# The row pitch of the pairs' split inputs and gated products: 448 columns or 416

## The chip, the cores and the metric

One core of one Trainium2 chip. The metric is the device time of the whole program in microseconds (us), the median of three runs. A profile is one execution, taken by the hardware profiler.

## What is computed

One layer of an encoder, in float32, applied with the same weights to 512 prompt tokens and 2048 sample tokens, each of 1024 features:

```python
h = rms(x, norm1_g)
q, k, v, c = split(h @ w_in)
attn = window_attention(rms(q), rms(k), v, sink)        # +-128 keys, ALiBi
u = silu(layernorm(dwconv31(a * sigmoid(gate))))        # a, gate = split(c)
x = x + concat(attn, u) @ w_out
h2 = rms(x, norm2_g)
g = silu(dwconv3(h2 @ ffn_w_gate) + ffn_dw_b)
x = x + (g * (h2 @ ffn_w_up)) @ ffn_w_down              # D_FF = 2816
```

What matters here is the last two lines, the feed-forward part.

## The kernel before, in words

**Splitting.** Every float32 matmul is done as three faster ones: an operand is split into a high part (a copy rounded by ScalarE, ACT) and a low part (input minus high part, by VectorE, DVE), and high x high, high x low and low x high are added up in PSUM. A matmul has a stationary operand of 128 x 128 and a moving one of 128 rows by up to 512 columns. Columns are tokens, so a tile is [128 partitions, rows of tokens], and TensorE (PE) reads one row of it per matmul.

**Stages.** The program is one list of slots of TensorE's work: projections and output products of five chunks of 512 tokens, with attention and convolution beside them, then the feed-forward part of two plain windows of 462 and 444 tokens (L2224, L2240), and from about 1483 us to the end two *pairs* of windows of TP = 414 tokens each. A window is loaded with one token more at each side, TQ = TP + 2 = 416, for the convolution over three tokens.

**The pairs.** For a pair the gate and up products of two windows, two halves of the features and two rows of weight tiles are made in Winograd's form of Strassen's scheme: seven products in place of eight. Its inputs are seven window parts, the loaded B11, B12, B21, B22 and the differences T1 to T4 (`pair_window_sum`, L1942; B12 and T3 share a buffer). Each is [128, KH = 4, TQ], split by ACT (`pair_window_high`, L1490) into `b_hi` and by DVE (`pair_window_low`, L1947) into `b_lo`. `pair_product` (L2370) makes one of the seven products: for each of four rows three matmuls, over columns 0 to 415 for the gate and 1 to 414 for up. ACT copies a product out of PSUM into `e_buf` (L1500), DVE adds others to it (L1954), then come the convolution's taps (L1963 and L1966, which read from one and two columns further on), the activation, the product of gate and up (L1978), and the split of the result into `mid2`: high part by ACT (`pair_mid_high`, L1530), low part by DVE (`pair_mid_low`, L1986). `mid2` is [128, 4 tiles, 2 parts, 2 windows, TP]. `pair_down` (L2384) multiplies it by the down weights, four or two tiles deep, and DVE adds the result to `pair_y` (L2000). Weight tiles of 512 columns are split at L1477 and L1930.

A pair is 22 groups (11 pairs of hidden tiles, gate and up) in six *passes*. A full pass is 336 product matmuls (four groups of seven products of twelve) and then 192 down matmuls.

**Order.** All four queues follow lists written by the planner for each product: `SP_AT`, `ACT_AT`, `DVE_AT` and the list of products `PROD`. They hold no address, and no size of a buffer enters them. Loads of window parts (`load_pair_window`, L942) for the second pair wait until the last group of the first pair has used the buffer; they read rows of 416 tokens from a scratch tensor in HBM where rows lie PAD_COLS apart. They share the queue of SyncE (SP) with the loads of weights (L957, L966).

**Places.** Tiles are put at offsets worked out from a base, which here is byte 7168 of the partition, a multiple of 256. The places before and after the pairs' stage overlap in time with other tiles, and two of them are maxima, in which the sizes of the pairs' buffers appear (L600 to L603):

```python
R_SM = max(R_Y + up256(4 * KT * TC), R_D + 4 * B_BYTES + 3 * E_BYTES + M_BYTES + 2 * Y_BYTES + V_BYTES)
R_HW = R_SM + up256(2 * up(4 * TH) + 2 * up(4 * TC))
R_SIDE = max(R_HW + 2 * up(4 * KT * H_PITCH), R_SM + (HI_RING + 5) * W_BYTES + 2 * V_BYTES + H)
```

With the kernel's numbers the first is max(125440, 123904) and the second max(165632, 163840). `pitch(cols)` rounds up to a multiple of 64 columns, 256 bytes. B_BYTES is the size of one window part (seven `b_lo`, which share their places with `b_raw`, and seven `b_hi`), M_BYTES that of `mid2`.

Of the kernel before, what the change touches and what calls it, by code (L numbers as in the profile page):

```python
# [45 lines left out]
TP = 414  # L46
# [6 lines left out]
TQ = TP + 2  # L53


def pitch(cols):
    return -(-cols // 64) * 64
# [473 lines left out]
def encoder_layer(nc, x, x_tok, w_in, w_out, w_ffn, w_down, w_pass, params, consts, y):  # L531
    with ExitStack() as ctx:
# [60 lines left out]
        def up256(n):  # L593
            return -(-n // 256) * 256

        B_PITCH, P_PITCH = pitch(TQ), pitch(TP)
        B_BYTES, E_BYTES, V_BYTES, W_BYTES, Y_BYTES = 4 * KH * B_PITCH, up256(4 * TQ), up256(4 * TP), 4 * KH * P, up256(4 * KT * TP)
        M_BYTES = 4 * 4 * 2 * 2 * P_PITCH
        M_PITCH, H_PITCH = pitch(TC), pitch(TH)
# [1935 lines left out]
```

## Time and profile before

| | |
|---|---|
| median of 3 runs | 2582.4 us (2579.91, 2582.4, 2582.7) |
| span of the profiled execution, first to last instruction | 2578.6 us |
| that execution's own time | not listed; its span is 3.8 us below the median |
| instructions | 35519 |
| TensorE, VectorE, ScalarE, GpSimd busy | 99%, 72%, 48%, 7% of the span |
| granted TensorE clock | 1.000 |

In a profile, PE is TensorE's matmuls, PEld its weight loads, DVE VectorE, ACT ScalarE, POOL GpSimd, SP SyncE; a q behind a name is that engine's queue. Line numbers are those of the kernel. Matmuls overlap: one of them lasts about twice the distance between two starts, so the pace is read from starts or from the chain, not from the mean of one. Tile names are given without their numbers, so `part_hi`, `T_hi` and `B_hi` each stand for several buffers.

### The profile page before, as it was taken

The page shows a single profiled execution, that of the slowest core. Times are in us where ns is not written, and L with a number is a line of the kernel's source. Part 1 is how long each engine was busy: PE and PEld are TensorE (multiplying, and loading weights), DVE is VectorE, ACT ScalarE, POOL GpSimd, SP SyncE. Part 2 cuts the span into 40 slices and gives each one's busy share as a digit, 9 for nine tenths or more (in the row PEclk, how much of TensorE's full clock was granted, in tenths as well). Part 3 has the DMA queues.
Part 4 walks back from the last instruction along what each step waited for, and adds up shares of the span by engine and source line. Part 5 has one row for each costly group of instructions (what it writes and reads, how often), then busy time and mean ns, then how long its engine had stood idle before and what let it go on. Part 6 is the DMA issues. An engine that isn't in the chain of part 4 may idle for free. (4 is left out here: it accounts for less than half of the span.)

```text
span 2578.6 us, 35519 instructions
## 1 busy us (share of the span) xinstructions
PE 2556.6 (99%) x12927; PEld 2287.9 (89%) x12927; DVE 1861.8 (72%) x3100; ACT 1250.3 (48%) x2166; POOL 184.7 (7%) x316
## 2 busy tenths in 40 slices
PE   8999999999999999999999999999999999999999
PEld 6877777788878887888888899999999999999999
DVE  4776658887888697968884687657667875765765
ACT  6345544468337844683563444335335443533532
POOL 0110021101011111110101100000000100000000
PEclk9999999999999999999999999999999999999999
DMA  9967789734554465447439542222223522221212
GB/s 350 348 229 237 261 290 345 276 112 164 205 206 137 146 246 212 162 159 263 155 122 357 178 148 68 66 60 68 66 61 116 171 66 62 66 66 61 67 58 70
DMA packets 139757, 419.11 MB, mean 163 GB/s; under 512 B 24160, under 2 KB 38880, under 8 KB 122944
## 3 DMA queue, kind: packets, MB, share of 16 engines
q1 hardware_dynamic: 113632, 317.93, 36.5%
q0 software_dynamic: 25952, 98.92, 10.0%
q8 instruction: 104, 1.70, 0.3%
q14 instruction: 69, 0.57, 0.1%
HBM read 328.01 MB, written 88.77 MB: 162 GB/s over the span
## 5 line engine op out<-in xcount | busy, mean ns | idle before, releaser
L1477 ACT ACTIVATE part_hi<-part_raw 128x512 fp32r<-128x512 f32 x396 | 247.6, 627 | 387.7 <-DMA part_raw<-w_pass_t 158.4
L2224 PE MATMUL bank<-hw_hi,weights 128*128 128x462 f32 (+3 forms) x1408 | 420.8, 373 | 0.0
L1751 DVE SCALAR_TENSOR_TENSOR cc<-win,par,cc 128x512 f32<-128x512 f32 x600 | 408.4, 745 | 0.0
L2384 PE MATMUL bank<-mid,part_hi 128*128 128x414 f32 x1408 | 376.9, 348 | 2.5 <-DVE mid L1986 2.0
L1930 DVE TENSOR_TENSOR part_lo<-part_raw,part_hi 128x512 fp32r<-128x512 f32 x396 | 271.0, 689 | 136.1 <-ACT part_hi L1477 130.6
L2175 PE MATMUL bank<-h_hi,weights 128*128 128x512 f32 x1104 | 354.6, 394 | 0.0
L2224 PEld LDWEIGHTS bank<-hw_hi,weights 128*128 128x128 f32 x1408 | 264.9, 188 | 37.0 <-issue 12.2
L2384 PEld LDWEIGHTS bank<-mid,part_hi 128*128 128x128 f32 x1408 | 263.3, 188 | 4.3 <-DVE mid L1986 3.4
L2224 PE MATMUL bank<-hw_lo,weights 128*128 128x464 f32 (+3 forms) x704 | 259.3, 368 | 0.0
L2175 PEld LDWEIGHTS bank<-h_hi,weights 128*128 128x128 f32 x1104 | 207.3, 188 | 51.2 <-issue 5.9
L2370 PE MATMUL bank<-T_hi,part_hi 128*128 128x414 f32 (+1 forms) x704 | 246.2, 350 | 0.5 <-DVE e L1954 0.5
L2370 PE MATMUL bank<-T_lo,part_hi 128*128 128x414 f32 (+1 forms) x704 | 246.0, 349 | 0.0
L2370 PE MATMUL bank<-T_hi,part_lo 128*128 128x414 f32 (+1 forms) x704 | 245.8, 349 | 0.0
L2000 DVE TENSOR_TENSOR pair_y<-bank,pair_y 128x414 f32<-128x414 f32 x192 | 111.9, 588 | 185.1 <-PE bank L2384 185.0
L2384 PE MATMUL bank<-mid,part_lo 128*128 128x414 f32 x704 | 245.0, 348 | 0.0
L1644 DVE TENSOR_TENSOR weights<-wraw,weights 128x1024 fp32r<-128x1024 f32 x154 | 187.9, 1221 | 55.6 <-ACT weights L1213 55.4
L2240 PE MATMUL bank<-mid,weights 128*128 128x462 f32 (+1 forms) x1056 | 223.9, 370 | 0.0
L2240 PEld LDWEIGHTS bank<-mid,weights 128*128 128x128 f32 x1056 | 197.1, 188 | 22.7 <-issue 5.0
L2175 PE MATMUL bank<-h_lo,weights 128*128 128x512 f32 x552 | 215.4, 390 | 0.0
L1213 ACT ACTIVATE weights<-wraw 128x1024 fp32r<-128x1024 f32 x154 | 162.9, 1058 | 93.6 <-DMA wraw<-w_down_t 67.4
L2209 PE MATMUL bank<-cat_hi,weights 128*128 128x512 f32 x640 | 204.1, 394 | 2.4 <-DMA cat_lo<-cat_scratch 2.4
L2370 PE MATMUL bank<-B_hi,part_hi 128*128 128x416 f32 (+1 forms) x528 | 184.4, 349 | 1.4 <-DVE yb L1905 1.4
(221 smaller groups left out, 4283.0 us busy)
## 6 DMA issues: line engine op xcount, KB each, us to landing
weights<-weight_scratch SPq DMA_DIRECT2D x88, 1024.0 KB, 6.0
wraw<-w_ffn_t SPq DMA_DIRECT2D x88, 512.0 KB, 3.5
part_raw<-w_ffn_t SPq DMA_DIRECT2D x176, 256.0 KB, 2.7
weight_scratch<-weights POOLq DMA_DIRECT2D x22, 1024.0 KB, 7.7
wraw<-w_down_t SPq DMA_DIRECT2D x44, 512.0 KB, 3.5
part_raw<-w_pass_t SPq DMA_DIRECT2D x88, 256.0 KB, 2.6
cat_hi<-cat_scratch SPq DMA_DIRECT2D x10, 1024.0 KB, 6.8
cat_lo<-cat_scratch SPq DMA_DIRECT2D x10, 1024.0 KB, 8.9
```

Of the source, the lines that this page charges most:

```text
L1213: nc.scalar.activation(whi[n % RING], wraw[n % RING][:], ACT.Copy).then_inc(s_whi, 1)
L1477: nc.scalar.activation(p_hi[k % HI_RING][:], p_raw[part_of(k)][:], ACT.Copy).then_inc(s_whi, 1)
L1644: nc.vector.tensor_tensor(wlo[n % RING], wraw[n % RING][:], whi[n % RING].bitcast(F32), ALU.subtract) \
L1751: nc.vector.scalar_tensor_tensor(acc, win[i][:, tap:tap + TB], w_tap, acc, ALU.mult, ALU.add).then_inc(s_cv, 1)
L1930: nc.vector.tensor_tensor(p_lo[part_of(k)][:], p_raw[part_of(k)][:], p_hi[k % HI_RING][:].bitcast(F32), ALU.subtract).then_inc(s_wlo, 1)
L2000: nc.vector.tensor_tensor(yb2[i][:, o, :], bank[BANK_Y[n % 4]][:, 0:TP], yb2[i][:, o, :], ALU.add) \
L2175: mm = nc.tensor.matmul(out[:], l[:, k, :], r[:, k, :], start=(k == 0 and i == 0), stop=(k == KT - 1 and i == 2))
L2209: mm = nc.tensor.matmul(out[:], l[:, k, :], r[:, k, :], start=(k == 0 and i == 0), stop=(k == KT - 1 and i == 2))
L2224: mm = nc.tensor.matmul(out, l[:, k, :], r[:, k, cols], start=(k == 0 and j == 0), stop=(k == KT - 1 and j == 2))
L2240: mm = nc.tensor.matmul(out, l[:, q, :], mid[:, k, part, 0:WIDTH[w]], start=(k == 0 and j == 0), stop=(k == FH - 1 and j == 2))
L2370: mm = nc.tensor.matmul(out, l[:, t, :], r[:, t, cols], start=(p in (1, 2, 5) and t == 0 and j == 0), stop=(t == KH - 1 and j == 2), skip_ ...
L2384: mm = nc.tensor.matmul(bank[BANK_Y[n % 4]][:, 0:TP], l[:, (deep * o + t) % KH, :], mid2[:, t, part, i, :], start=(t == 0 and z == 0), sto ...
```

## The change

The distance between two rows of a window part, and between two rows of `mid2`, is rounded up to 16 columns (64 bytes) in place of 64 columns (256 bytes). TQ = 416 and TP = 414 columns both had a pitch of 448 and have 416 now. The plain windows' M_PITCH and H_PITCH stay as they are.

```diff
-        B_PITCH, P_PITCH = pitch(TQ), pitch(TP)
+        B_PITCH, P_PITCH = -(-TQ // 16) * 16, -(-TP // 16) * 16
         B_BYTES, E_BYTES, V_BYTES, W_BYTES, Y_BYTES = 4 * KH * B_PITCH, up256(4 * TQ), up256(4 * TP), 4 * KH * P, up256(4 * KT * TP)
         M_BYTES = 4 * 4 * 2 * 2 * P_PITCH
```

## Rows read from the trace of the kernel before

**Rows 1.** The page: engine busy us (share) xinstructions; the granted clock in 40 slices.

```profile
PE 2556.6 (99%) x12927; PEld 2287.9 (89%) x12927; DVE 1861.8 (72%) x3100; ACT 1250.3 (48%) x2166; POOL 184.7 (7%) x316
...
PEclk9999999999999999999999999999999999999999
```

**Rows 2.** The page: the chain that ended last, share of the span by line.

```profile
PE bank L2370 24%; PE bank L2384 15%; DVE v L1978 0%; DVE part_lo L1930 0%; ACT part_hi L1477 0%; DVE mid L1986 0%; DMA part_raw<-w_ffn_t 0%; ACT mid L1530 0%; DVE e L1954 0%; DVE v L1963 0%; DVE part_raw L1921 0%; ACT v L1519 0%; DVE pair_y L2000 0%; ACT e L1500 0%; DVEq L1953 0%
```

**Rows 3.** The chain in order of time: start us, us, what, matmuls.

```profile
1639.82 63.04 PE bank L2370 x336
1702.86 35.84 PE bank L2384 x192
...
1997.65 32.99 PE bank L2384 x174
2030.64 42.70 PE bank L2370 x228
```

**Rows 4.** TensorE's waits, 1400 us to the end: us in total, times, longest.

```profile
PE bank L2384 <- DVE mid L1986: 2.0, 4, 1.0
...
PE bank L2384 <- DVE pair_y L2000: 0.5, 1, 0.5
```

**Rows 5.** Groups by shape, TensorE: count, busy us, mean ns of one.

```profile
L2384 PE MATMUL bank<-mid,part_hi 128*128 128x414 f32 x1408 | 376.9, 348 | 2.5 <-DVE mid L1986 2.0 <-DVE pair_y L2000 0.5
...
L2370 PE MATMUL bank<-T_lo,part_hi 128*128 128x416 f32 x352 | 123.5, 351 | 0.0
...
L2370 PE MATMUL bank<-T_lo,part_hi 128*128 128x414 f32 x352 | 122.5, 348 | 0.0
```

**Rows 6.** Timeline of TensorE: start us, us; firsts and lasts of stretches without a break.

```profile
1343.38 0.36 PE L2224 MATMUL bank<-hw_lo,weights 128*128 128x446 f32 x1
...
1346.98 0.36 PE L2224 MATMUL bank<-hw_lo,weights 128*128 128x446 f32 x1
...
1686.95 0.35 PE L2370 MATMUL bank<-B_hi,part_hi 128*128 128x414 f32 x1
...
1689.19 0.35 PE L2370 MATMUL bank<-B_hi,part_hi 128*128 128x414 f32 x1
...
1693.67 0.35 PE L2370 MATMUL bank<-B_hi,part_hi 128*128 128x416 f32 x1
...
1695.93 0.35 PE L2370 MATMUL bank<-T_hi,part_hi 128*128 128x416 f32 x1
```

**Rows 7.** Window parts, tile B_raw: duration ns min/median/max, first and last start.

```profile
L1490 ACT ACTIVATE B_hi<-B_raw x6: 1577/1578/1592, 1443.0 to 2011.9; 128x1664 fp32r<-128x1664 f32 x6
L1947 DVE TENSOR_TENSOR B_lo<-B_raw,B_hi x6: 1880/1885/1891, 1448.2 to 2024.6; 128x1664 fp32r<-128x1664 f32 x6
...
DMA to landing us min/median/max: 4.8/6.4/11.2
```

**Rows 8.** Lines L1477 and L1930, the same columns.

```profile
L1477 ACT ACTIVATE part_hi<-part_raw x396: 612/631/640, 1468.4 to 2560.7; 128x512 fp32r<-128x512 f32 x198
...
L1930 DVE TENSOR_TENSOR part_lo<-part_raw,part_hi x396: 679/691/695, 1482.1 to 2567.2; 128x512 fp32r<-128x512 f32 x198
```

**Rows 9.** Lines L1986, L1963 and L1966, the same columns.

```profile
L1986 DVE TENSOR_TENSOR mid<-v,mid x88: 581/583/591, 1516.2 to 2542.2; 128x414 fp32r<-128x414 f32 x88
...
L1963 DVE SCALAR_TENSOR_TENSOR v<-e,par,v x66: 643/646/650, 1498.2 to 2524.5; 128x414 f32<-128x414 f32 x66
...
L1966 DVE SCALAR_TENSOR_TENSOR v<-e,par,v x66: 650/651/653, 1498.8 to 2525.2; 128x414 f32<-128x414 f32 x66
```

**Rows 10.** Timelines of SP, ACT and DVE at the change of pairs.

```profile
1988.69 0.38 SPq L942 DMA_DIRECT2D T_raw<-h_scratch  x1
...
1997.40 1.58 ACT L1490 ACTIVATE B_hi<-B_raw 128x1664 fp32r<-128x1664 f32 x1
...
1999.59 1.88 DVE L1942 TENSOR_TENSOR T_raw<-T_raw,B_raw 128x1664 f32<-128x1664 f32 x1
...
2003.60 0.59 DVE L2000 TENSOR_TENSOR pair_y<-bank,pair_y 128x414 f32<-128x414 f32 x1 [1.63 <-PE bank L2384]
```

## The prediction

> **What bounds the kernel now.** I read the page first. TensorE is busy for 2556.6 of the 2578.6 us of the span, and its clock is at the top digit in all 40 slices [rows 1]; nothing else comes near. The chain that ended last, followed back as far as the view goes, is 24% of the span products of the pairs (L2370) and 15% down products of the pairs (L2384); no other line has as much as 1% [rows 2]. These two lines are also the only matmuls that read what the change moves. The chain in order of time says the same more sharply: a pass is 336 product matmuls in 63.04 us and then 192 down matmuls in 35.84 us, one behind the other with no other piece between them [rows 3]. TensorE's list of waits from 1400 us to the end has four entries, from 2.0 down to 0.5 us [rows 4]. So in the last 1100 us the time is the number of matmuls times the pace at which they start. There are 3696 products (six groups of 352 and six of 264) and 2112 down matmuls (1408 and 704), of which [rows 5] show three groups, 5808 together; 5808 x 187.3 ns = 1088 us.
>
> The pace: 63.04 / 336 = 187.6 ns and 35.84 / 192 = 186.7 ns [rows 3]. It follows the columns: 18 matmuls of 446 columns take 3.60 us from start to start, 200.0 each [rows 6]. Against 186.7 at 414 columns that is 0.42 ns for each column more (13.3 / 32), one period of the 2.4 GHz that the full granted clock means, and some 14 ns that do not depend on them. So reading the moving operand is on the path, and anything that slows it shows in full; there is no slack to hide it.
>
> **The change, part by part.** Only the distance between rows changes: 448 columns (1792 bytes) become 416 (1664 bytes). B_BYTES goes from 7168 to 6656, M_BYTES from 28672 to 26624. No instruction, wait, shape, buffer or queue entry is added or removed. 14 x 512 + 2048 = 9216 bytes come free, and nothing takes them. The two places where the pairs' layout could push other things, R_SM and R_SIDE, are maxima whose other term was already the larger (125440 against 123904; 165632 against 163840), so every buffer outside the pairs' stage stays where it was. Each buffer of the pairs still begins at a multiple of 256 bytes, since 6656, 26624 and the other sizes are such multiples. What is new is inside: 1664 is 6.5 x 256, so every second row begins 128 bytes past a multiple of 256.
>
> *Moving reads.* In a window part, rows 1 and 3 of four are such rows: half of the 3696 products. In mid2 the row number is (tile, part, window), so these are all rows of the second window: half of the 2112. Together 1848 + 1056 = 2904 matmuls. No row of the trace has this start, so I bound it. The nearest rows are the up products: they read columns 1 to 414, so they start 4 bytes past the multiple. 12 of them take 2.24 us, 186.7 each [rows 6], just what a down matmul with 414 columns from an aligned start takes; both forms have a mean of 348 ns [rows 5]. An odd start as such costs 0. The other end is one step of the pace seen between widths: from 414 to 446 columns, 13.3 ns, as if half a block of 256 bytes more were read; 2904 x 13.3 = 38.6 us. Even if the memory were read in whole blocks of 256 bytes, a row at offset 128 with 416 columns reaches byte 1792 and touches 7 blocks, and an aligned one touches 7 too; with 64- or 128-byte blocks the counts are 26 and 13 in both layouts. I take 0, the up products' value. Below 0: the gate products (416 columns) run at 2.26 us for 12, 188.3 ns [rows 6], where 2 columns more than 414 would explain 187.5; if the new layout brought all products to 186.7, the gain would be 3696 x 0.9 = 3.3 us. For small losses, the slowest stretch of down matmuls is 174 in 32.99 us, 189.6 ns [rows 3]; all 2112 at that pace would add 6.1 us. Both ends stay for the range.
>
> *Splitting and differences of windows.* L1490, L1942 and L1947 now see four rows that touch each other: one run of 1664 elements. If ending a row cost something, this would save it. L1947 takes 1885 ns for four rows of 416 [rows 7], L1930 takes 691 for 512 elements [rows 8]: (1885 - 691) / 1152 = 1.036 ns per element, which leaves 161 ns fixed, for one row as for four. ACT: 1578 against 631 [rows 7, 8], 0.822 per element, 210 fixed. Nothing is there to save; at most 28 splits and 8 differences in the whole kernel are touched, and the pair of windows that is split in mid-run (1997 to 2032 us) is ready without a wait of TensorE at 2030.64 [rows 3]. Term 0, cover: down matmuls of the last pass.
>
> *Writes to mid2.* L1986 takes 583 ns, 88 times, and ACT's L1530 writes the same rows just before it [rows 9]. Half will write at offset 128. For a start off the multiple the trace has VectorE's reads at 4 and 8 bytes, 646 and 651 ns, so some 5 ns [rows 9]. TensorE waited for L1986 four times, 2.0 us in all [rows 4]; 4 x 5 ns is nothing. Term 0, for the rest the cover is the products of the next group.
>
> *Window loads.* Eight transfers of 832 KB, the B ones 4.8 / 6.4 / 11.2 us from issue to landing [rows 7], now write their odd rows from offset 128. Packets stay one row, since the source rows are apart in HBM. Those of the second pair are issued before 1991 us. The tightest is B12 (loaded into T_raw, issued at 1988.69), which VectorE reads at 1999.59, 10.9 us later, without having idled [rows 10]; the first split, at 1997.40, is of B11, loaded earlier still [rows 10]. Were it 1 us late, VectorE would stand for 1 us, but 1.63 us of idle time follow before 2003.60 [rows 10]. Term 0, from 0 to 1 us. The Trainium skill speaks against the change here (DMA: Bandwidth & Descriptors, How a descriptor splits into AXI transactions): a descriptor that does not start at 256 bytes starts its first transaction at the boundary below. An estimate from its table: 56 beats for such a row in place of 52. No row here shows it for a write into SBUF; by it these loads would be some 4% longer on average, and the sum still 0.
>
> *Sum:* 0. The profiled execution has a span of 2578.6 us; its own time is not listed, and the median of the three runs, 2582.4, lies 3.8 us above that span. So 2582.4.
>
> **Rivals.** 0.2%, 5.2 us, is about what a measurement of this kernel can tell from no change.
>
> *Slower: TensorE reads a row slower when it starts 128 bytes past a multiple of 256.* Place: every second row in L2370, every second-window matmul in L2384. Price 13.3 ns on 2904, 38.6 us: 2621. It decides from 5.2 us / 2904 = 1.8 ns per such matmul. For it: reading is on the path, and no row excludes this one offset. Against it: the up products at 4 bytes pay nothing, and the block counts are equal. 0.11.
>
> *Faster: the pace of the products falls to that of the down matmuls,* 3.3 us: 2579. That alone is within 0.2%; it needs another 1.9 us, as from TensorE's idle pieces between 1981 and 1998 us. For it: gate products are 0.8 ns above what their columns explain. Against it: nothing in the change touches a column count. Over the line 0.04.
>
> *The change does not do what it says:* TQ = 416 divides by 16, TP = 414 rounds up to 416, so the pitch does fall; but had the freed bytes moved other buffers, the plain stage would shift too. The maxima above exclude it. The time would be the same, and it is in the forecast's chance.
>
> **Numbers.** Same 0.84, slower 0.12 (the rival, and 0.01 for the 6.1 us of slow down matmuls), faster 0.04. The range takes the bounds of the small unknowns around 2582.4: down by 3.3 us and the 2.5 us by which the lowest of the three runs lies below the median, 2576.6; up by 6.1 and the 1 us of the loads, 2589.5. It leaves out the rival at 2621.
>
> **What would show it.** Right: L2370 and L2384 keep means of 351, 348 and 348 ns, a pass stays 63.04 + 35.84 us, L1947 and L1490 stay at 1885 and 1578, the starts of the passes shift by less than 2 us. Wrong: down matmuls of the two windows with different paces, or products with rows 1 and 3 slower than 0 and 2; a pass longer by 336 / 2 x 13.3 = 2.2 us and 1.3 us; or new waits of TensorE near 1998 to 2030 us for L1942 or a window load.

## The result and the profile after

The changed kernel takes 2587.8 us (2586.0 to 2590.1 in ten runs) against 2582.5 (2579.9 to 2585.6 in ten runs): 1.0022 of the time before, with a 95% interval of 1.0014 to 1.0030. It is slower by some 5 us, clear of the noise. The forecast was no change; the time lies inside its range (2576.6 to 2589.5), near the upper end. The profiled execution has a span of 2588.2 us.

The page's engine row, the columns as in [rows 1]:

```profile
PE 2565.8 (99%) x12927; PEld 2289.1 (88%) x12927; DVE 1862.7 (72%) x3100; ACT 1250.5 (48%) x2166; POOL 184.7 (7%) x316
```

The counts are the same, VectorE and ScalarE are busy for the same time within 1 us, and TensorE is busy for 9 us more. TensorE stands for 22 us in both profiles (2578.6 less 2556.6, and 2588.2 less 2565.8), so no wait was added; its own work takes longer. The chain in order of time, as [rows 3]:

```profile
1534.35 13.72 PE bank L2384 x72
...
1643.13 63.69 PE bank L2370 x336
1706.82 35.90 PE bank L2384 x192
...
2003.56 32.81 PE bank L2384 x174
2036.37 43.18 PE bank L2370 x228
```

A pass takes 63.69 us of products in place of 63.04, and 35.91 of down matmuls in place of 35.84; every full pass shows the same two numbers to 0.01 us. That is 1.93 ns more for each of the 3696 products, 7.1 us, and 0.36 ns for each of the 2112 down matmuls, 0.8 us. The first of these passes starts at 1643.13 in place of 1639.82; of these 3.3 us 0.4 belong to the pairs' stage, and the rest had gathered before it, in stages that the change does not touch. The groups by shape and the timeline, as [rows 5, 6]:

```profile
L2384 PE MATMUL bank<-mid,part_hi 128*128 128x414 f32 x1408 | 377.7, 349 | 2.1 <-DVE mid L1986 1.7 <-DVE pair_y L2000 0.4
...
L2370 PE MATMUL bank<-T_lo,part_hi 128*128 128x414 f32 x352 | 123.7, 351 | 0.0
L2370 PE MATMUL bank<-T_hi,part_hi 128*128 128x416 f32 x352 | 123.7, 351 | 0.0
L2370 PE MATMUL bank<-T_lo,part_hi 128*128 128x416 f32 x352 | 123.4, 351 | 0.0
```

```profile
1693.00 0.35 PE L2370 MATMUL bank<-B_hi,part_hi 128*128 128x414 f32 x1
...
1695.28 0.35 PE L2370 MATMUL bank<-T_hi,part_hi 128*128 128x414 f32 x1
...
1697.56 0.35 PE L2370 MATMUL bank<-B_hi,part_hi 128*128 128x416 f32 x1
...
1699.84 0.35 PE L2370 MATMUL bank<-T_hi,part_hi 128*128 128x416 f32 x1
```

Twelve up products (414 columns) take 2.28 us, 190.0 ns each, where they took 186.7; twelve gate products (416) take 2.28 in place of 2.26. The mean duration of a single matmul hardly shows it (351 in place of 348), since matmuls overlap. The distance between starts does. Below, a *pace* is the mean of these distances over all matmuls of a form (one line and one number of columns), with the few distances of 230 ns or more left out, where TensorE stands or turns to something else.

The side work came out as forecast: the rows that answer to [rows 7] moved by no more than 4 ns in the median, and the window loads land in 7.2 us in place of 6.4 with nothing waiting for them.

```profile
L1490 ACT ACTIVATE B_hi<-B_raw x6: 1577/1582/1593, 1445.7 to 2017.8; 128x1664 fp32r<-128x1664 f32 x6
L1947 DVE TENSOR_TENSOR B_lo<-B_raw,B_hi x6: 1879/1883/1885, 1451.4 to 2030.5; 128x1664 fp32r<-128x1664 f32 x6
...
DMA to landing us min/median/max: 4.7/7.2/11.2
```

### The profile page after: what moved, and what is told of

It is laid out like the page before. It is cut to its first block and busy times, and to the rows that moved or that the text cites. A ratio compares the mean times of both kernels' runs of the same rounds, so it can differ in the third digit from the quotient of the medians.

```text
span 2588.2 us, 35519 instructions
## 1 busy us (share of the span) xinstructions
PE 2565.8 (99%) x12927; PEld 2289.1 (88%) x12927; DVE 1862.7 (72%) x3100; ACT 1250.5 (48%) x2166; POOL 184.7 (7%) x316
## 5 line engine op out<-in xcount | busy, mean ns | idle before, releaser
L1477 ACT ACTIVATE part_hi<-part_raw 128x512 fp32r<-128x512 f32 x396 | 247.7, 627 | 398.4 <-DMA part_raw<-w_pass_t 158.6
L1930 DVE TENSOR_TENSOR part_lo<-part_raw,part_hi 128x512 fp32r<-128x512 f32 x396 | 270.6, 688 | 141.2 <-ACT part_hi L1477 134.7
L1644 DVE TENSOR_TENSOR weights<-wraw,weights 128x1024 fp32r<-128x1024 f32 x154 | 187.9, 1220 | 56.7 <-ACT weights L1213 56.5
```

Source lines behind the costliest of these rows:

```text
L1477: nc.scalar.activation(p_hi[k % HI_RING][:], p_raw[part_of(k)][:], ACT.Copy).then_inc(s_whi, 1)
L1644: nc.vector.tensor_tensor(wlo[n % RING], wraw[n % RING][:], whi[n % RING].bitcast(F32), ALU.subtract) \
L1930: nc.vector.tensor_tensor(p_lo[part_of(k)][:], p_raw[part_of(k)][:], p_hi[k % HI_RING][:].bitcast(F32), ALU.subtract).then_inc(s_wlo, 1)
```

## The experiments

A run of the chip has a spread of a few us, but within one profile the full passes repeat to 0.01 us, in every kernel but one (the shift by 64, below). So the verdicts rest on the pass and the pace, from one profile of each kernel, and the time stands beside them. *Start* means the first byte of a row that is read, counted from the last multiple of 256. There were three theories at first: A, a start of 128 costs; B, a change of the start from row to row costs; C, the distances between buffers, which shrank with the pitch, cost. D and E (what is special about a start) and F and G (the moving row against the weights, or alone) came later and are told in the expectations.

### Which part of the change

```diff
-        B_PITCH, P_PITCH = -(-TQ // 16) * 16, -(-TP // 16) * 16
+        B_PITCH, P_PITCH = -(-TQ // 16) * 16, pitch(TP)
```

> Window parts at a pitch of 416 columns, the gated products (mid2) back at 448. The changed kernel's pass is 63.69 us of products and 35.91 of down matmuls, against 63.04 and 35.84 before. All theories that put the loss on the products' reads expect 63.7 and 35.84 here and a time near 2587. If the loss comes from the writes to mid2 or from the places of the weights behind it, products fall back to 63.04 and the time to 2582.5.

Measured: 2590.1 us, ratio 1.0031 (1.0021 to 1.0041). The chain in order of time:

```profile
1646.70 63.69 PE bank L2370 x336
1710.39 35.85 PE bank L2384 x192
```

The products keep their loss to the hundredth, and the down matmuls are back at 35.85. The loss is that of the window parts' pitch; the pitch of mid2 costs 0.06 us a pass.

### Where the rows start, in which order, and where the buffers lie

All rows 128 bytes on, at the old pitch (the same shift for `b_lo` and `b_hi`; what lies behind the parts is moved by 256):

```diff
+        SHIFT, PAD = 128, 256
...
-            b_raw[b] = run(lo_at[b], (f"{b}_raw", [P, KH, B_PITCH], F32))[0][:, :, 0:TQ]
+            b_raw[b] = run(SHIFT + lo_at[b], (f"{b}_raw", [P, KH, B_PITCH], F32))[0][:, :, 0:TQ]
```

> Pitch of 448 as before, but every window part begins 128 bytes further on, so that all four rows start 128 bytes past a multiple of 256 and none at one. Theory A, a row that starts 128 bytes off costs more to read: rows 1 and 3 cost the changed kernel 0.65 us a pass, so four such rows cost 1.3 us, 64.3 us of products and about 2596. Theory B, it is the change of the start from row to row that costs: no change here, 63.04 us and 2582.5. Theory C, the distances between buffers that shrank with the pitch: they are as before, 63.04 us and 2582.5.

Measured: 2587.7 us, ratio 1.0024 (1.0013 to 1.0035). The chain, where the line numbers are one higher than before:

```profile
1641.57 63.75 PE bank L2371 x336
1705.32 35.84 PE bank L2385 x192
```

A start at 128 costs by itself, without any change from row to row: up products (start 132) 190.9 ns, gate (start 128) 188.7. That is against B as the sole cause. It is not A's doubling either: 0.71 us and not 1.3.

The changed kernel with another order of rows:

```diff
-                for t in range(KH):
+                for t in (0, 2, 1, 3):
```

> The changed kernel with the four rows of a product taken in the order 0, 2, 1, 3: the starts go 0, 0, 128, 128 in place of 0, 128, 0, 128. Theory A: the same rows are read, 63.69 us and 2587.8. Theory B: two changes of start in four rows in place of four, about 63.35 us and 2585. Theory C: 63.69 us and 2587.8.

Measured: 2588.3 us, ratio 1.0024 (1.0012 to 1.0036). The chain, and the timeline at one product of 12, six matmuls of rows 0 and 2 and six of rows 1 and 3:

```profile
1644.40 63.54 PE bank L2370 x336
1707.94 35.91 PE bank L2384 x192
```

```profile
1694.15 0.36 PE L2370 MATMUL bank<-B_hi,part_hi 128*128 128x414 f32 x1
...
1695.28 0.35 PE L2370 MATMUL bank<-B_hi,part_hi 128*128 128x414 f32 x1
...
1696.43 0.36 PE L2370 MATMUL bank<-T_hi,part_hi 128*128 128x414 f32 x1
```

The first six take 1.13 us and the last six 1.15: rows 1 and 3 are the dear ones, over all up products 191.0 ns against 187.5. Fewer changes of start save 0.15 of the 0.65 us, so A carries most and B a part.

Pitch 416, every buffer with the room it had before:

```diff
-        B_BYTES, ... = 4 * KH * B_PITCH, ...
-        M_BYTES = 4 * 4 * 2 * 2 * P_PITCH
+        B_BYTES, ... = 4 * KH * pitch(TQ), ...
+        M_BYTES = 4 * 4 * 2 * 2 * pitch(TP)
```

> Pitch of 416 as in the changed kernel, but each buffer keeps the room and so the place that it had at 448; the freed bytes lie unused behind each. Theories A and B: 63.69 us a pass of products and about 2587.8. Theory C, the distances between the buffers: 63.04 us and 2582.5.

Measured: 2587.1 us, ratio 1.0021 (1.0011 to 1.0031), the changed kernel's numbers:

```profile
1642.10 63.69 PE bank L2370 x336
1705.79 35.90 PE bank L2384 x192
```

C falls.

### Other starts

The next four ask what is special about a start. The first leaves the pitch at 448 and puts a row's data at column 31 (for `b_lo` and `b_hi` too):

```diff
-            b_raw[b] = run(lo_at[b], (f"{b}_raw", [P, KH, B_PITCH], F32))[0][:, :, 0:TQ]
+            b_raw[b] = run(lo_at[b], (f"{b}_raw", [P, KH, B_PITCH], F32))[0][:, :, 31:31 + TQ]
```

> Pitch 448, places as before, but the data of a window part begins at column 31 of its row: the gate products read from 124 bytes past a multiple of 256, the up products from exactly 128. With all rows 128 bytes on, the up products (start 132) took 190.9 ns and the gate products (128) 188.7, against 187.0 (4) and 188.1 (0) before. Theory D, few columns are left in the first 256 bytes (32 or 31 of 64): up stays at about 190.8, gate rises to about 191. Theory E, what costs is a start that is neither at a multiple of 128 nor near one of 256, that is, the 4 bytes on top of 128: up falls to 187 as the down matmuls that start at 128 (187.0), gate rises since it is now the one off 128; the sum stays near 63.7 us a pass or above.

The second and third are the shift above with `SHIFT` 64 and 192 in place of 128:

> Pitch 448, every window part 64 bytes further on: gate reads start at 64, up reads at 68. Theory D: 48 and 47 columns are left in the first 256 bytes, between the 64 of before and the 32 of the shift by 128, so up about 189 ns and a pass 63.4 us. Theory E: up pays the same as at 132, about 190.9 ns, and a pass takes 63.7 us.

> Pitch 448, every window part 192 bytes further on: gate reads start at 192, up reads at 196. Theory D: only 16 and 15 columns are left in the first 256 bytes, so the price is above that of a shift by 128: up about 193 ns, gate about 190, a pass 64.3 us, 2594. Theory E: as at 132, up 190.9 ns, a pass 63.7 us, 2588.

The fourth is the changed kernel with `B_PITCH = 432`:

> Pitch of 432 columns for the window parts (rows start at 0, 192, 128 and 64 past a multiple of 256), mid2 at 416. Theory D: the mean over the four starts, about as the changed kernel or somewhat worse, 63.7 to 63.9 us a pass; rows 1 and 2 dear, row 0 free. Theory E: three of four rows off, so dearer than the changed kernel's two of four: 64.0 us a pass, 2591.

Measured: the first takes 2577.8 us, ratio 0.9983 (0.9973 to 0.9992): faster than both kernels. Start 64: 2583.6 us, 1.0008 (0.9998 to 1.0017). Start 192: 2584.8 us, 1.0010 (1.0000 to 1.0019). Pitch 432: 2589.0 us, 1.0027 (1.0018 to 1.0036). The chain of the first:

```profile
1643.61 62.68 PE bank L2370 x336
1706.29 35.84 PE bank L2384 x192
```

and of the fourth:

```profile
1639.93 63.75 PE bank L2370 x336
1703.68 35.91 PE bank L2384 x192
```

The paces at pitch 448, by start:

| run | up start, pace | gate start, pace | products of a pass |
|---|---|---|---|
| kernel before | 4, 187.0 ns | 0, 188.1 ns | 63.04 us |
| shift 64 | 68, 187.8 | 64, 188.2 | 63.13 |
| data from column 31 | 128, 186.4 | 124, 186.7 | 62.68 |
| shift 128 | 132, 190.9 | 128, 188.7 | 63.75 |
| shift 192 | 196, 190.7 | 192, 186.8 | 63.44 |

D expected the fewest columns in the first 256 bytes to be dearest for both forms; the gate at 192, with 16 left, is one of the cheapest entries. The 63.75 us at pitch 432 are what D expected, but the paces at 192 are against it. E had the up read at 128 right, which is 4.5 ns cheaper than the one at 132. It expected the gate read at 124 to rise, which fell, and 68 to cost as 132 does; in the table it costs 3 ns less. So neither theory holds as it stands, and what remains is a table.

The entry at 68 hides something. In that profile the same work, with the same places, takes two different times:

```profile
1548.17 58.43 PE bank L2371 x312
1606.61 36.09 PE bank L2385 x192
...
2095.22 59.04 PE bank L2371 x312
2154.26 35.84 PE bank L2385 x192
```

In the 312 products from 2095.22 us the up pace is 190.0 ns, in the first 228 of the stage it is 191.2, and in all other stretches 186.7 or 187.6. So at this start the place does not fix the pace alone, and E fails only for the larger part of the products. In the other kernels whose paces stand here the up pace of every stretch stays within 1 ns.

### The moving row alone, or its place against the weights

The weight loads overlap the matmuls: PEld is busy for 89% of the span and PE for 99% [rows 1]. So one row may be read while the next stationary operand is loaded. Here the kernel before keeps its window parts, and only the pairs' weight tiles go 128 bytes further on (the `v` buffers behind them move by 256):

```diff
-            p_raw[k], = run(o, (f"part{i}_raw", [P, KH, P], F32))
-            p_lo[k], = run(o, (f"part{i}_lo", [P, KH, P], F32R))
-        p_hi = [run(o, (f"part_hi{i}", [P, KH, P], F32R))[0] for i, o in enumerate(w_hi_at)]
+            p_raw[k], = run(128 + o, (f"part{i}_raw", [P, KH, P], F32))
+            p_lo[k], = run(128 + o, (f"part{i}_lo", [P, KH, P], F32R))
+        p_hi = [run(128 + o, (f"part_hi{i}", [P, KH, P], F32R))[0] for i, o in enumerate(w_hi_at)]
```

> The kernel before, window parts at 0 past a multiple of 256 and a pitch of 448, but the pairs' weight tiles (high, low and raw) 128 bytes further on. Theory F, the pace hangs on where a moving row lies against the weights that are loaded meanwhile: the distance is that of the run with all window parts at 128, so up products 190.9 ns, gate 188.7, 63.7 us a pass. Theory G, it hangs on the moving row alone: 187.0, 188.1 and 63.04 us as before.

Then both together:

> The kernel before with window parts and weight tiles of the pairs both 128 bytes further on. Each alone made the up products 190.8 ns and a pass 63.6 to 63.8 us. Theory F, the distance between the moving row and the weights loaded meanwhile sets the pace: it is that of the kernel before, so 187.0 and 188.1 ns, 63.04 us, 2582. Theory G, each start costs by itself: the two losses together or one of them, 63.7 us or more, 2588 or more.

Measured: weights alone 2590.0 us, 1.0030 (1.0016 to 1.0045). Both 2581.9 us, 0.9999 (0.9989 to 1.0009). The chain with the weights moved:

```profile
1643.80 63.63 PE bank L2370 x336
1707.44 35.85 PE bank L2384 x192
```

and with both moved:

```profile
1641.58 63.04 PE bank L2371 x336
1704.62 35.84 PE bank L2385 x192
```

This decides between F and G. Moving the weights slows the up products to 190.8 ns though each window part is where it was, and moving both gives 187.0, 188.3 and 63.04 us back. All other buffers stayed at multiples of 256 in both runs, so it is not the place against one of them. For the up products it is the place of the moving row against the stationary tile, modulo 256 bytes, that makes the difference. It is shown for a change of that distance by 128 bytes alone. The gate products bear it out only in part: 188.1 ns before, 188.7 with the parts moved, 187.9 with the weights moved, where F expected 188.7. The down matmuls do not: with the weights moved their distance is 128 too, and their pass stays at 35.85 us. In the changed kernel rows 1 and 3 change that distance by 128 bytes, because the weight tiles' rows kept their pitch of 512. A changed kernel in which those rows of the weight tiles follow was not run.

One rule of the Trainium skill reads otherwise (SBUF — State Buffer, Who interferes with whom): it gives TensorE two independent read ports, one for the moving operand and one for weight loads, and says that only the port pair shared by VectorE and GpSimd causes contention. By it the place of the weights should not matter to the moving read. The traces here differ: 187.0 against 190.8 ns when the weights are moved. The measurement decides; which circuit is behind it no run here shows.

### Versions with the better start

The changed kernel's pitch of 416 with data from column 31 (each part has 256 bytes more, so 5.5 KB are free in place of 9):

```diff
+            def rows_of(at, name, dt):
+                t = run(at, (name, [P, KH * B_PITCH + 31], dt))[0]
+                return t[:, 31:31 + KH * B_PITCH].rearrange("p (k n) -> p k n", k=KH)[:, :, 0:TQ]
```

> The changed kernel's pitch of 416 for both, but the data of each window part begins 31 columns into its buffer: gate rows start at 124 and 252 past a multiple of 256 in turn, up rows at 128 and 0. Frees 5.5 KB in place of 9. If the gain of the start at 124 and 128 (62.68 us a pass, against 63.04 before) belongs to up reads at a multiple of 128, it stays here: 62.7 us, and with mid2 at 35.91 us about 2579. If a change of start from row to row costs by itself, as the order 0, 2, 1, 3 suggested (63.54 against 63.69), 63.2 us and 2584.

Measured: 2582.2 us, 1.0006 (0.9997 to 1.0015), the time of the kernel before:

```profile
1643.82 63.00 PE bank L2374 x336
1706.82 35.90 PE bank L2388 x192
```

63.00 lies between the two expectations (62.7 and 63.2): up starts of 128 and 0 in turn run at 187.8 ns, above the 186.4 of 128 alone. Then the plain windows, on top of the fast version at pitch 448; `hw_lo` and `hw_raw` are changed as `hw_hi` is, and the last line is in the second run alone:

```diff
-        hw_hi = run(R_HW, ("hw_hi", [P, KT, H_PITCH], F32R))[0][:, :, 0:TH]
+        hw_hi = run(R_HW, ("hw_hi", [P, KT, H_PITCH], F32R))[0][:, :, 31:31 + TH]
...
-        mid = run(R_MID, ("mid", [P, FH, 2, M_PITCH], F32R))[0][:, :, :, 0:TC]
+        mid = run(R_MID, ("mid", [P, FH, 2, M_PITCH], F32R))[0][:, :, :, 32:32 + TC]
```

> The fast version (pitch 448, data from column 31, 2577.8 us) with the plain windows' split inputs also from column 31 of their 512: up reads start at 128, gate reads at 124. Before, matmuls of 462 to 464 columns there start 209 to 213 ns apart, 14 ns above their columns would be 207. If the start helps as in the pairs, 3 ns on half or all of 2112 matmuls: 3 to 6 us, 2573. If it depends on the length of the row, no change or a loss of the same size.

> As the run before, and the plain windows' gated products from column 32 of 512, so that the down matmuls (L2240) start at 128 and not at 0. Before they are 211.7 ns apart at 462 columns and 200.0 at 444. For down matmuls of the pairs a start at 128 changed nothing (187.0 and 187.0), so I expect no change against the run before at 444 and at most 3 ns less on 528 matmuls at 462, 1.6 us.

Measured: 2575.6 us, 0.9977 (0.9968 to 0.9986), and 2570.6 us, 0.9960 (0.9948 to 0.9973). The groups by shape in the kernel before:

```profile
L2240 PE MATMUL bank<-mid,weights 128*128 128x462 f32 x528 | 115.8, 377 | 0.0
L2224 PE MATMUL bank<-hw_hi,weights 128*128 128x462 f32 x352 | 108.3, 378 | 0.0
L2240 PE MATMUL bank<-mid,weights 128*128 128x444 f32 x528 | 108.2, 364 | 0.0
L2224 PE MATMUL bank<-hw_hi,weights 128*128 128x464 f32 x352 | 107.7, 377 | 0.0
```

and in the second version:

```profile
L2240 PE MATMUL bank<-mid,weights 128*128 128x462 f32 x528 | 113.4, 372 | 0.0
L2240 PE MATMUL bank<-mid,weights 128*128 128x444 f32 x528 | 107.8, 363 | 0.0
L2224 PE MATMUL bank<-hw_hi,weights 128*128 128x462 f32 x352 | 106.9, 375 | 0.0
L2224 PE MATMUL bank<-hw_hi,weights 128*128 128x464 f32 x352 | 106.6, 373 | 0.0
```

Down matmuls of 462 columns went from 211.6 to 206.8 ns, up products of 462 (`hw_hi`) from 211.7 to 206.8, gate products of 464 from 209.0 to 206.7. At the narrower window gate products of 446 went from 201.1 to 198.4, up products of 444 from 202.2 to 201.1 (199.9 in the first version), and down matmuls of 444 from 200.0 to 199.3. My expectation of at most 1.6 us for `mid` was too low: 528 x 4.8 ns is 2.5 us. From the first plain matmul to the last the profiles show 968.0 us before, 963.5 in the first version and 961.3 in the second. The ratio of the first version lies only 0.0006 below that of the start at column 31 alone (0.9983), within both intervals, so its gain is shown by the trace and not by the time. Last, both together at the small pitch:

> The changed kernel's pitch of 416 with window parts from column 31, and the plain windows' inputs from column 31 and gated products from column 32. The pairs' stage as in the run with pitch 416 from column 31 (63.00 us a pass, 35.90), the plain stage as in the run with both plain changes, which took 10 us off the kernel before, some 6 of them in the plain stage: about 2575, faster than the kernel before by 0.2 to 0.3% with 5.5 KB free.

Measured: 2574.9 us, 0.9972 (0.9962 to 0.9982). It keeps 5.5 KB of the room and is faster than both kernels; at pitch 448 the gain is larger, 0.40%. The two intervals overlap, but the passes agree: 63.00 and 35.90 us here against 62.68 and 35.84.

## Why the prediction was wrong

**What held.** The bound (TensorE, starts one behind another without slack), the pace as the thing to watch, the byte counts, the two maxima that leave the other stages alone, the splits, the window loads and the waits all came out as written. The statement that anything that slows the moving read shows in full is borne out in the main: 7.9 us by the full passes, 6.8 us more from the first matmul of the stage to its last in the profile, and a median 5.3 us up (3.6 to 7.7 by the interval). The expected form of failure was named too, a slower row at 128, with rows 1 and 3 dearer than 0 and 2; it had a chance of 0.11 and a price of 13.3 ns.

**The step that failed** is the term for moving reads: "An odd start as such costs 0", and "I take 0, the up products' value". The up products of before start 4 bytes past a multiple of 256 while their weights start at one, a distance of 4. That row says nothing of a distance of 132, and at that distance all up products cost 3.9 ns more. The argument by counts of blocks failed with it, since the same row of the same length reads at 187.0 or 190.8 ns depending on where the *weights* lie. I had bounded one operand's address where the quantity is a relation between two that are read together.

**The sizes.** The loss is 7.9 us / 2904 = 2.7 ns for each matmul with a moved start, above the 1.8 from which I said the rival decides and a fifth of its upper end. It is uneven: up products +2.8 ns over all four rows, gate +1.2, down +0.36. The down matmuls, 1056 of my 2904, hardly count. The small bounds I kept for the range (6.1 us for a slower stretch of down matmuls) did not come about. That the range held the time is luck: it did so by a term that had nothing to do with the loss. That term also read its row too high. The 189.6 ns of [rows 3] hold one distance of 294 ns; the others of that stretch average 188.1.

**The Trainium skill's rule on descriptors** (DMA: Bandwidth & Descriptors, How a descriptor splits into AXI transactions) gave, as an estimate, 4% on the window loads. Their median landing went from 6.4 to 7.2 us, and to 6.7 in the run with the parts alone at the small pitch. The six transfers spread from 4.7 to 11.2 us, so these rows neither bear the rule out nor refute it. TensorE waited for none of them.

## What to carry to other kernels

Where TensorE is the bound, treat the start of each moving row modulo 256 bytes and that of the stationary tile as one tuning parameter: a view that begins some columns further on costs nothing but padding, and here such views, in the pairs and the plain windows together, were worth 0.4%. Read the effect in the distance between starts over a repeated stretch of one profile, which shows 0.01 us in 63 (and compare the repeats, since one kernel here had more than one pace at the same places), and not in the total time or in the mean duration of one matmul. When an edit "only" packs a layout, ask for every operand that is read on the critical path at the same time what the edit does to their places against each other.

## What the hardware showed that was not expected

- TensorE's pace for 414 columns ranged from 186.4 to 190.9 ns by placement alone; for 462 columns from 206.8 to 211.7 ns.
- Alternating starts seem to cost something of their own: 187.8 ns for up starts of 128 and 0 in turn, where 128 alone gives 186.4 and down matmuls of the same width run at 186.7 from 0. No run has up reads from 0 alone.
- The places alone do not fix the pace. In the run with all parts at 64 the down matmuls took 36.09 us a pass, though their rows and weights lay where they lay in the runs with 128 and 192, which took 35.84. Only the products before them differed, and one stretch of the same run, from 2154.26 us, took 35.84. These are two paces of one kind of work, 188.0 and 186.7 ns. Both also occur in the kernel before: its 174 down matmuls from 1997.65 us run at 188.1, its full passes at 186.7. What switches between them is open, and so is why an up read at 128 is cheaper than the gate reads at 128 or the up reads at 132; other distances than those in the table were not tried.
- Moving the weights by 128 was not in all ways the same as moving the parts: gate products 187.9 against 188.7 ns, a pass 63.63 against 63.75 us. The distance modulo 256 explains the large part of the effect and not every tenth.
